# Seven products for eight: the up and gate projections of both feed-forwards formed from sums of weight blocks and of input halves

## The chip, the core and the metric

The kernel runs on one NeuronCore of one Trainium2 chip. The engines work side by side, each through its own program in order, and wait for one another on semaphores: TensorE (PE, matrix products), VectorE (DVE), ScalarE (ACT), GpSimd (POOL), and SyncE (SP), which issues most of the transfers from memory. The metric is the time of one execution in microseconds on the device; less is better.

## What is computed

The program is three blocks of a network on 512 tokens of width 1024, in f32. The change touches the gated feed-forward `conv_ffn`, which occurs twice (l = 0 after the gMLP mixer, l = 1 after the attention); the rest is left as it is. D_FF is 2816, so that `w_in` has 22 blocks of 128 columns for up and 22 for gate.

```python
def conv_ffn(h, w_in, conv_w, conv_b, w_down):
    a = h @ w_in
    C = a.shape[-1]
    a = lax.conv_general_dilated(
        a, conv_w[:, None, :].astype(a.dtype), window_strides=(1,),
        padding=[(CONV_WIDTH - 1, 0)], dimension_numbers=('NWC', 'WIO', 'NWC'),
        feature_group_count=C) + conv_b
    up, gate = jnp.split(a, 2, axis=-1)
    return (jax.nn.silu(gate) * up) @ w_down
```

Between them the kernel also computes, during the first feed-forward, the modulation vector of the third block, `mod = silu(c) @ ada_w + ada_b`, a product of one vector of 1024 with a matrix of 1024 by 6144.

## The kernel before

Activations are held turned: 128 channels on the partitions, 512 tokens along a row, `hT[:, k, :]` for the eight blocks k of 128 input channels (KB = 8). A **unit** n of a feed-forward (22 of them, FB = 22) is one block of 128 output channels of up and the same of gate. For each unit SP brings 1 MB of weights, in two transfers of 512 KB (`unit_loads`), into one of two slots of a ring; slot j = n mod 2. In the loops i counts pairs of units and j the unit in a pair, n = 2i + j. Waits go by counts, so that the order of each engine's program and the counts set all that happens.

- **PE** (`feed_forward` on `pe`, L910): per unit two products of 8 matmuls each, 128x128 weights against 512 columns, accumulated over k in bank 2j + b (b = 0 up, b = 1 gate). Each f32 matmul of the source is two MATMUL rows in the profile. Unit 0 is made by `raw_products` (L874) from the input before its norm is known. PE waits for the ring's load and for `ff_tap0`, which says that the bank was read two units ago. In l = 0, `ada_unit` (L839) follows each unit: two matmuls of one column that finish modulation unit n - 1.
- **ACT** (L1657, L1664): per bank the middle tap of the convolution with scale and bias, from PSUM to `conv`; then, for a pair of units, the two silu of the gates into `sil`.
- **DVE** (L2059, L2064, L2072): per bank the two outer taps, which multiply the shifted bank and add into `conv`; then gate times up into `act`. L2107 adds the bias to the two columns of modulation.
- **POOL** (`ada_unit`, L661, L663): in l = 0 only. For each of 24 modulation units it waits for a load of 1 MB, multiplies it by silu(c) broadcast (L661, 128x2048), and adds the eight blocks in a tree (L663, 1024, 512, 256 columns). Nothing of the feed-forward itself runs on POOL.
- **SP** (L443, L461): per unit the two ring transfers, once PE has freed the slot, and in l = 0 the modulation weights, once PE has made `ada_unit(n - 2)`.

After the units comes the down projection (L849, `linear`), whose first block waits for `act` block by block and whose blocks 0, 2 and 4 are followed by the last three modulation units.

## Time and profile before

| | us |
|---|---|
| median of 3 runs | 2788.99 |
| lowest, highest | 2786.19, 2789.99 |
| the profiled execution | 2788.59 |
| its span, first to last instruction | 2786.5 |
| PE busy in the span | 2626.5 (94%) |
| DVE, ACT, POOL busy | 842.5, 581.8, 442.4 |
| matmuls of L910 (both feed-forwards, units 1 to 21) | 582.1 |

The profile of one execution records every instruction with its start and length. "Busy" is the share of time in which an engine has an instruction in it. Matmuls are pipelined: the length of one (592 ns at 512 columns) is longer than the distance from one to the next, which is what counts and is read from a stretch of many. A small share of matmul records can be missing. Each row says what its engine waited for when it sat idle before.

### The profile page before, as it was taken

The numbers are of one execution on the slowest core, as the hardware profiler recorded it, in microseconds if no ns is written. First come the engines' busy times: TensorE is split into PE (matmuls) and PEld (weight loads), VectorE is DVE, ScalarE is ACT, GpSimd is POOL, SyncE is SP. The second block draws the span as 40 slices with busy tenths as digits, with TensorE's granted clock in tenths as the row PEclk, the third lists the DMA queues.
The fourth block names the chain that finished last, engine by engine and source line by source line (L and its number), as shares of the span: only waits on it lengthen the run. The fifth ranks groups of instructions, "written<-read, shape, count | busy, mean of one in ns | idle before, by whom it ended". The sixth has DMA issues, their size and how long they took to land. (4 is left out here: it accounts for less than half of the span.)

```text
span 2786.5 us, 27348 instructions
## 1 busy us (share of the span) xinstructions
PE 2626.5 (94%) x9893; PEld 1364.1 (49%) x9893; DVE 842.5 (30%) x1970; ACT 581.8 (21%) x1086; POOL 442.4 (16%) x403
## 2 busy tenths in 40 slices
PE   6999999999999999999999989999999999999992
PEld 6554444444566444444445446567655444444440
DVE  1023222102333232221022335565633323322215
ACT  2111111101333211110024542222113111111111
POOL 3015555400000100000112101011100111111110
PEclk9999999999999999999999999999998999999996
DMA  7224555432122122223322111000115799999985
GB/s 158 70 76 137 149 151 151 138 83 66 46 61 61 61 76 75 75 75 83 83 65 82 53 40 35 25 16 15 38 49 228 288 421 413 386 409 407 394 349 218
DMA packets 290655, 404.48 MB, mean 145 GB/s; under 512 B 14418, under 2 KB 253736, under 8 KB 264432
## 3 DMA queue, kind: packets, MB, share of 16 engines
q1 hardware_dynamic: 273808, 366.24, 38.1%
q0 software_dynamic: 15632, 34.44, 3.8%
q10 hardware_dynamic: 1104, 2.31, 0.2%
q8 instruction: 71, 1.16, 0.2%
q14 instruction: 40, 0.33, 0.0%
HBM read 396.20 MB, written 27.71 MB: 152 GB/s over the span
## 5 line engine op out<-in xcount | busy, mean ns | idle before, releaser
L910 PE MATMUL bank<-hT,bring 128*128 128x512 f32 x1344 | 582.1, 593 | 0.0
L910 PEld LDWEIGHTS bank<-hT,bring 128*128 128x128 f32 x1344 | 253.8, 190 | 311.9 <-issue 311.9
L849 PE MATMUL bank<-bring 128*128 128x512 f32 x704 | 303.3, 593 | 0.0
L1554 PE MATMUL bank<-bring 128*64 128x512 f32 (+1 forms) x512 | 226.8, 596 | 1.1 <-ACT bring L1974 0.8
L849 PEld LDWEIGHTS bank<-bring 128*128 128x128 f32 x704 | 133.5, 190 | 166.5 <-issue 166.5
L2059 DVE SCALAR_TENSOR_TENSOR ffw<-bank,col,ffw 128x511 f32<-128x511 f32 x88 | 65.9, 749 | 413.6 <-ACT ffw L1657 413.4
L1657 ACT ACTIVATE ffw<-bank,col 128x512 f32<-128x512 f32 x88 | 68.4, 777 | 492.8 <-PE bank L910 470.1
L2044 DVE TENSOR_TENSOR xT<-bank,xT 128x512 f32<-128x512 f32 x32 | 22.1, 692 | 370.5 <-PE bank L849 370.4
L1554 PEld LDWEIGHTS bank<-bring 128*64 128x64 f32 (+1 forms) x512 | 77.9, 157 | 96.2 <-issue 96.2
L1567 PE MATMUL bank<-bring,xT 128*64 128x512 f32 (+1 forms) x256 | 117.2, 600 | 5.7 <-DMA two<-exp_w_down 3.1
L646 POOL TENSOR_TENSOR ysq<-ysq 128x512 f32<-128x512 f32 x23 | 29.2, 1270 | 582.1 <-ACT ysq L1629 516.7
L1113 PE MATMUL bank<-hT,bring 128*128 128x512 f32 x256 | 115.8, 599 | 2.2 <-DVE ysq L2217 2.2
L1989 ACT ACTIVATE xT<-bank 128x256 f32<-128x256 f32 x44 | 16.9, 384 | 467.6 <-PE bank L1554 467.6
L1554 PE MATMUL bank<-two,bring 128*64 128x512 f32 (+1 forms) x256 | 113.4, 596 | 0.1
L1554 PE MATMUL bank<-ysq,bring 128*64 128x512 f32 (+1 forms) x256 | 113.4, 596 | 0.0
L740 POOL TENSOR_TENSOR ffw<-two,maskT 128x512 f32<-128x512 f32 x40 | 52.2, 1313 | 383.6 <-DVE two L2391 316.3
L2603 DVE TENSOR_TENSOR xT<-bank,ysq 128x512 f32<-128x512 f32 x88 | 60.8, 691 | 170.7 <-PE bank L1567 170.7
L661 POOL TENSOR_TENSOR two<-two,csil 128x2048 f32<-128x2048 f32 x24 | 86.5, 3603 | 155.6 <-DMA two<-ada_w 138.4
L663 POOL TENSOR_TENSOR two<-two 128x1024 f32<-128x1024 f32 (+2 forms) x72 | 104.0, 1444 | 5.7
L1208 PE MATMUL bank<-hT,bring 128*128 128x512 f32 x192 | 92.4, 617 | 2.4 <-ACT bring L1849 2.4
L2599 DVE TENSOR_TENSOR xT<-bank,xT 128x256 f32<-128x256 f32 x44 | 18.7, 424 | 239.1 <-ACT xT L1989 239.1
L792 POOL DMA_INDIRECT y_dram<-xT,slot_row x44 | 43.9, 998 | 203.1 <-DVE xT L2603 194.4
(498 smaller groups left out, 3603.1 us busy)
## 6 DMA issues: line engine op xcount, KB each, us to landing
bring<-f_w_in SPq DMA_DIRECT2D x88, 512.0 KB, 5.2
bring<-exp_w_gate SPq DMA_DIRECT2D x32, 1024.0 KB, 11.3
bring<-exp_w_up SPq DMA_DIRECT2D x32, 1024.0 KB, 18.4
bring<-exp_w_down SPq DMA_DIRECT2D x32, 1024.0 KB, 20.4
two<-ada_w SPq DMA_DIRECT2D x24, 1024.0 KB, 5.3
bring<-f_w_down SPq DMA_DIRECT2D x16, 1408.0 KB, 7.0
two<-exp_w_gate SPq DMA_DIRECT2D x16, 1024.0 KB, 10.9
two<-exp_w_up SPq DMA_DIRECT2D x16, 1024.0 KB, 18.1
```

Of the source, the lines that this page charges most:

```text
L661: step(1, nc.gpsimd.tensor_tensor(w, w, csil[:].unsqueeze(2).to_broadcast([P, KB, 256]), ALU.mult))
L663: step(k, nc.gpsimd.tensor_tensor(w[:, 0:n, :], w[:, 0:n, :], w[:, n:2 * n, :], ALU.add))
L740: nc.gpsimd.tensor_tensor(Am[h], ABT[h][:, :, 0:P], bc4(maskT[n][:]), ALU.mult)\
L849: mm = pe.matmul(ps[BANKS[stage][n % 4]][:], w[:, k, n % per * P:(n % per + 1) * P], rhs[:, k, :], start=(k == 0), stop=(k == kb - 1))
L910: mm = pe.matmul(ps[2 * j + b][:], w[:, k, b * P:(b + 1) * P], hT[:, k, :], start=(k == 0), stop=(k == KB - 1))
L1113: mm = pe.matmul(ps[n % 2][:], slot(n // 2, 8, 256)[:, k, n % 2 * P:(n % 2 + 1) * P], hT[:, k, :], start=(k == 0), stop=(k == KB - 1))
L1208: mm = pe.matmul(ps[(0, 7, 6)[m]][:], w, hT[:, k, :], start=(k == 0), stop=(k == KB - 1))
L1554: mm = pe.matmul(ps[3][m * h:m * h + m, :].rearrange("p (m n) -> p m n", m=2), hgT[par][:, k, m * h:m * h + m], w, start=(k == 0), stop=(k ...
L1567: mm = pe.matmul(ps[5 + half][m * h:m * h + m, :], eactT[par][:, k * P + m * h:k * P + m * h + m], exw[b][:, 4096 + k * D + half * 512:409 ...
L1657: nc.scalar.activation(conv[j][b], ps[2 * j + b][:], ACT.Identity, scale=col[:, bass.ds(c0 + P + blk, 1)], bias=col[:, bass.ds(c0 + P + 44 ...
L2059: nc.vector.scalar_tensor_tensor(out=c[:, 1:T], in0=ps[2 * j + b][:, 0:T - 1], scalar=col[:, bass.ds(c0 + 44 + blk, 1)], in1=c[:, 1:T], op ...
L2603: return nc.vector.tensor_tensor(yrow[par][:, cols], ps[5 + half][:], g2_row[:, cols], ALU.mult)
```

## The change

The 22 up and gate blocks keep their units. From unit 2 on, a unit's product is taken as a 2 by 2 product of blocks: the weights are split by input channels (k 0 to 3, k 4 to 7) and by up and gate, the inputs by input channels and by halves of the tokens (0 to 255, 256 to 511). Seven products of such blocks stand for the eight, each of 4 matmuls of 128x128 weights against 256 columns (`product`). Units 0 and 1 are made as before. What is new for this:

- `tsum`: four sums of input blocks (128x1024 each), made once per feed-forward by DVE, kept in a part of `ysq`.
- `wsum7`: four sums of weight blocks (128x512 each), made for every unit by POOL in `weight_sums`, in two buffers by j.
- PE's unit: 8 matmuls into bank a, 4 into d, 8 into b, 8 into c (two sets of four banks by j, `BANKS7`); it waits for the unit's weight sums (`ff_sum`) and for the bank set (`ff_step`).
- ACT copies the first product to SBUF (`p1_sb`); DVE makes up and gate in SBUF (`full`, in `AR2`) with seven adds of 256 columns; the taps of ACT and DVE then read `full` and not PSUM.
- The multiplication of the modulation weights by silu(c) moves from POOL to ACT (`ada_scale`, eight instructions of 256 columns with a scale per partition), at the end of each unit of l = 0. POOL keeps the tree.
- SP frees a ring slot after bank d, the second of the four.

The diff, cut: lines that go away on PE, ACT and DVE are those printed above.

```diff
+        tsum = [ysq[:, 1024 * n:1024 * n + 1024].rearrange("p (k t) -> p k t", k=4) for n in range(4)]
+        wsum7 = [[ysq[:, KB * T + 2048 * j + 512 * n:KB * T + 2048 * j + 512 * n + 512].rearrange("p (k n) -> p k n", k=4)
+                  for n in range(4)] for j in range(2)]
+        p1_sb, u2, u3 = rstd[:, 0:256], rms[:, 0:256], rms[:, 256:512]
...
+        full = [AR2[:, 0:512], AR2[:, 512:1024]]
...
+        FF_PRODS, FF_STEPS = 4 + 4 * (FB - 2), 8 + 9 * (FB - 2)
+        prods_at = lambda l, p: FF_PRODS * l + 4 + 4 * p
+        steps_at = lambda l, p: FF_STEPS * l + 8 + 9 * p
+        ADA_LATE = 2
+        acted_at = lambda l, p: 8 + 5 * p if l == 0 else 8 + 5 * (FB - 2) + ADA_LATE + 6 + 4 * p
+        BANKS7 = ((5, 4, 6, 7), (0, 3, 1, 2))
...
+                            if stage in ("f0in", "f1in"):
+                                sp.wait_ge(S[used], base + 2 + 2 * j if isinstance(i, int) else base + 8 * i - 10 + 4 * j)
...
-            def ada(i, first):
-                for j in range(2):
-                    ada_unit(2 * i + j, j)
-            def ada_unit(u, j):
-                def step(k, ins):
-                    ins.then_inc(s("ada_summed"), 1)
-                    if k < 4:
-                        settle(pool, s("ada_summed"), 4 * u + k)
+            def ada_unit(u, j, acted):
                 w = adaw[j]
-                settle(pool, s(f"ada{j}_loaded"), 16 * (u // 2) + 16 if isinstance(u, int) else 8 * (u - j) + 16)
-                step(1, nc.gpsimd.tensor_tensor(w, w, csil[:].unsqueeze(2).to_broadcast([P, KB, 256]), ALU.mult))
-                for k, n in ((2, 4), (3, 2), (4, 1)):
-                    step(k, nc.gpsimd.tensor_tensor(w[:, 0:n, :], w[:, 0:n, :], w[:, n:2 * n, :], ALU.add))
+                settle(pool, s("ff_acted"), acted)
+                for k, n in enumerate((4, 2, 1)):
+                    if k:
+                        settle(pool, s("ada_summed"), 3 * u + k)
+                    nc.gpsimd.tensor_tensor(w[:, 0:n, :], w[:, 0:n, :], w[:, n:2 * n, :], ALU.add).then_inc(s("ada_summed"), 1)
+            def weight_sums(l, i, j):
+                p = 2 * i + j - 2
+                _, base, d, *_ = plan[f"f{l}in"]
+                settle(pool, (S["ring0_loaded"], S["ring1_loaded"])[j], base[j] + 16 * d[j] * (i + 1))
+                if isinstance(p, int) and p < 2:
+                    pool.wait_ge(s("norm_ss_ready"), nth(f"f{l}"))
+                else:
+                    settle(pool, s("ff_prod"), prods_at(l, p - 2) + 4)
+                w, (s1, s2, s3, s4) = slot(j, 8, 256), wsum7[j]
+                at = 4 * ((FB - 2) * l + p)
+                nc.gpsimd.tensor_tensor(s1, w[:, 0:4, P:], w[:, 4:8, P:], ALU.add).then_inc(s("ff_sum"), 1)
+                nc.gpsimd.tensor_tensor(s3, w[:, 0:4, 0:P], w[:, 0:4, P:], ALU.subtract).then_inc(s("ff_sum"), 1)
+                settle(pool, s("ff_sum"), at + 1)
+                nc.gpsimd.tensor_tensor(s2, s1, w[:, 0:4, 0:P], ALU.subtract).then_inc(s("ff_sum"), 1)
+                settle(pool, s("ff_sum"), at + 3)
+                nc.gpsimd.tensor_tensor(s4, w[:, 4:8, 0:P], s2, ALU.subtract).then_inc(s("ff_sum"), 1)
+            def weight_side(l):
+                def body(i):
+                    for j in range(2):
+                        weight_sums(l, i, j)
+                        if l == 0:
+                            ada_unit(2 * i + j, j, acted_at(0, 2 * i + j - 2) + 5)
+                body(1)
+                with pool.Fori(2, FB // 2) as i:
+                    body(i)
...
-            looped(pool, ADA // 2, ada)
+            ada_unit(0, 0, 1)
+            ada_unit(1, 1, 8)
+            weight_side(0)
             for u in range(ADA, ADA_UNITS):
-                ada_unit(u, u % 2)
...
+                def product(bank, half, weights, rhs):
+                    for k in range(4):
+                        mm = pe.matmul(ps[bank][:, 256 * half:256 * half + 256], weights[:, k, :], rhs[:, k, :],
+                                       start=(k == 0), stop=(k == 3))
+                    return mm
+                def body(i):
                     for j in range(2):
+                        p = 2 * i + j - 2
+                        a, d, b, c = BANKS7[j]
+                        w, (s1, s2, s3, s4), (t1, t2, t3, t4) = slot(j, 8, 256), wsum7[j], tsum
                         ring_ready(pe, stage, i, j)
...
+                        pe.wait_ge(s("ff_sum"), 4 * ((FB - 2) * l + p) + 4)
+                        if not isinstance(p, int):
+                            pe.wait_ge(s("ff_step"), steps_at(l, p - 2) + 7)
+                        elif p == 0:
+                            pe.wait_ge(s("ff_step"), FF_STEPS * l + 4)
+                        else:
+                            pe.wait_ge(s("ff_tap0"), 44 * l + 4)
+                        product(a, 0, w[:, 0:4, 0:P], hT[:, 0:4, 0:256])
+                        product(a, 1, w[:, 4:8, 0:P], hT[:, 4:8, 0:256]).then_inc(s("ff_prod"), 1)
+                        if l == 0:
+                            ada_unit(2 * i + j - 1, 1 - j, ps[d][:, 256:258])
+                        product(d, 0, w[:, 4:8, P:], t4).then_inc(s("ff_prod"), 1)
+                        product(b, 0, s2, t2)
+                        product(b, 1, s3, t3).then_inc(s("ff_prod"), 1)
+                        product(c, 0, s1, t1)
+                        product(c, 1, s4, hT[:, 4:8, 256:512]).then_inc(s("ff_prod"), 1)
...
+                def ada_scale(u, j):
+                    settle(act_e, s(f"ada{j}_loaded"), 16 * (u // 2) + 16 if isinstance(u, int) else 8 * (u - j) + 16)
+                    for k in range(KB):
+                        ins = nc.scalar.activation(adaw[j][:, k, :], adaw[j][:, k, :], ACT.Copy, scale=csil[:, k:k + 1])
+                    ins.then_inc(s("ff_acted"), 1)
+                def middle_tap(src, j, b, blk):
+                    nc.scalar.activation(conv[j][b], src, ACT.Identity,
+                                         scale=col[:, bass.ds(c0 + P + blk, 1)],
+                                         bias=col[:, bass.ds(c0 + P + 44 + blk, 1)]).then_inc(s("ff_acted"), 1)
+                def gate(n, j):
+                    settle(act_e, s("ff_tap0"), 44 * l + 2 * n + 2)
+                    nc.scalar.activation(sil[j], conv[j][1], ACT.Silu).then_inc(s("ff_acted"), 1)
...
+                def body(i):
                     for j in range(2):
+                        n = 2 * i + j
+                        p = n - 2
+                        settle(act_e, s("ff_prod"), prods_at(l, p) + 1)
+                        if not isinstance(p, int) or p > 0:
+                            settle(act_e, s("ff_step"), steps_at(l, p - 1) + 2)
+                        nc.scalar.copy(p1_sb, ps[BANKS7[j][0]][:, 0:256]).then_inc(s("ff_acted"), 1)
+                        settle(act_e, s("ff_step"), steps_at(l, p) + 7)
+                        settle(act_e, s("ff_act"), FB * l + n - 1)
                         for b in range(2):
...
+                            middle_tap(full[b], j, b, n + 22 * b)
+                        gate(n, j)
+                        if l == 0:
+                            ada_scale(n, j)
...
+                h = [[hT[:, 4 * r:4 * r + 4, 256 * c:256 * c + 256] for c in range(2)] for r in range(2)]
+                s0 = FF_STEPS * l
+                dve.wait_ge(s("norm_h_ready"), h_count(f"f{l}", KB - 1))
+                nc.vector.tensor_tensor(tsum[0], h[0][1], h[0][0], ALU.subtract).then_inc(s("ff_step"), 1)
+                nc.vector.tensor_tensor(tsum[2], h[1][1], h[0][1], ALU.subtract).then_inc(s("ff_step"), 1)
+                dve.wait_ge(s("ff_step"), s0 + 1)
+                nc.vector.tensor_tensor(tsum[1], h[1][1], tsum[0], ALU.subtract).then_inc(s("ff_step"), 1)
+                dve.wait_ge(s("ff_step"), s0 + 3)
+                nc.vector.tensor_tensor(tsum[3], tsum[1], h[1][0], ALU.subtract).then_inc(s("ff_step"), 1)
...
+                def body(i):
                     for j in range(2):
...
+                        n = 2 * i + j
+                        p = n - 2
+                        a, d, b, c = [ps[x] for x in BANKS7[j]]
+                        prod, step, acted = prods_at(l, p), steps_at(l, p), acted_at(l, p)
+                        up, gate = full
+                        lo, hi = slice(0, 256), slice(256, 512)
+                        settle(dve, s("ff_acted"), acted + 1)
+                        nc.vector.tensor_tensor(up[:, lo], p1_sb, a[:, hi], ALU.add).then_inc(s("ff_step"), 1)
+                        settle(dve, s("ff_prod"), prod + 3)
+                        nc.vector.tensor_tensor(u2, p1_sb, b[:, lo], ALU.add).then_inc(s("ff_step"), 1)
+                        settle(dve, s("ff_step"), step + 2)
+                        nc.vector.tensor_tensor(u3, u2, b[:, hi], ALU.add).then_inc(s("ff_step"), 1)
+                        settle(dve, s("ff_step"), step + 3)
+                        nc.vector.tensor_tensor(gate[:, lo], u3, d[:, lo], ALU.subtract).then_inc(s("ff_step"), 1)
+                        if l == 0:
+                            ada_unit(n - 1, d[:, 256:258])
+                        settle(dve, s("ff_prod"), prod + 4)
+                        nc.vector.tensor_tensor(up[:, hi], u2, c[:, lo], ALU.add).then_inc(s("ff_step"), 1)
+                        nc.vector.tensor_tensor(gate[:, hi], u3, c[:, lo], ALU.add).then_inc(s("ff_step"), 1)
+                        settle(dve, s("ff_step"), step + 5)
+                        nc.vector.tensor_tensor(up[:, hi], up[:, hi], c[:, hi], ALU.add).then_inc(s("ff_step"), 1)
+                        settle(dve, s("ff_step"), step + 7)
+                        for b2 in range(2):
+                            outer_taps(full[b2], n, j, b2, acted + 2 + b2, step + 8 + b2)
+                        gated(n, j, acted + 4)
```

Unit n waits on POOL for `ff_acted` at `acted_at(0, n - 2) + 5`, that is 8 + 5(n - 2) + 5. ACT counts one up for the copy, two for the middle taps, one for the silu and one for the last instruction of `ada_scale(n)`: five a unit, 8 before unit 2.

**POOL, the loop of the first feed-forward.** Before, one unit (names: `two` holds the modulation weights, `csil` silu(c)):

```order
L661 TENSOR_TENSOR two<-two,csil 128x2048 [waits consts,ada0_loaded]
L52 ISA
L663 TENSOR_TENSOR two<-two 128x1024 [waits consts,ada_summed]
L52 REGISTER_ALU
L663 TENSOR_TENSOR two<-two 128x512 [waits consts,ada_summed]
L52 REGISTER_ALU
L663 TENSOR_TENSOR two<-two 128x256 [waits consts,ada_summed]
```

And now, one unit and the beginning of the next (`bring` holds the ring, `ysq` the weight sums):

```order
L694 TENSOR_TENSOR ysq<-bring 128x512 [waits consts,ff_prod]
L695 TENSOR_TENSOR ysq<-bring 128x512
L52 ISA
L697 TENSOR_TENSOR ysq<-ysq,bring 128x512 [waits consts,ff_sum]
L52 REGISTER_ALU
L699 TENSOR_TENSOR ysq<-bring,ysq 128x512 [waits consts,ff_sum]
L52 ISA
L681 TENSOR_TENSOR two<-two 128x1024 [waits consts,ff_acted]
L52 ISA
L681 TENSOR_TENSOR two<-two 128x512 [waits consts,ada_summed]
L52 REGISTER_ALU
L681 TENSOR_TENSOR two<-two 128x256 [waits consts,ada_summed]
```

What was a wait for a transfer ahead of L661 is a wait for ACT ahead of L681, and the weight sums of the next unit (L694 again) stand behind it.

**ACT, the first feed-forward.** Before, units 0 and 1 and the beginning of the loop (`ffw` holds `conv` and `sil`), with nothing between the silu and the next unit's taps:

```order
L1657 ACTIVATE ffw<-bank,col 128x512 [waits raw_scaled,ff_prod] x2
L1657 ACTIVATE ffw<-bank,col 128x512 [waits ff_prod] x2
L1664 ACT_TABLE_LOAD
L1664 ACTIVATE ffw<-ffw 128x512 [waits ff_tap0] x2
L80 UNCONDITIONAL_BRANCH
L80 ISA
L52 ISA [waits consts,ff_prod]
L1657 ISA [waits consts,ff_act]
L1657 ACTIVATE ffw<-bank,col 128x512
```

Now, unit 2, ahead of the loop (`rstd` is `p1_sb`, `AR2` is `full`):

```order
L1757 COPY rstd<-bank5 128x256 [waits ff_prod]
L1728 ACTIVATE ffw<-AR2,col 128x512 [waits ff_act,ff_step]
L1728 ACTIVATE ffw<-AR2,col 128x512
L1734 ACTIVATE ffw<-ffw 128x512 [waits ff_tap0]
L1724 ACTIVATE two<-two,csil 128x256 [waits ada0_loaded]
L1724 ACTIVATE two<-two,csil 128x256 x7
```

The scaling of the modulation weights (L1724) has come in behind the silu of the same unit.

**PE, the loop of the first feed-forward.** Before, one unit:

```order
L906 ISA [waits ring0_loaded]
L910 MATMUL bank<-hT,bring 128x512 [waits ff_tap0]
L910 MATMUL bank<-hT,bring 128x512 x7
L906 REGISTER_ALU
L910 MATMUL bank<-hT,bring 128x512 [waits ff_tap0]
L910 MATMUL bank<-hT,bring 128x512 x7
L836 ISA
L839 MATMUL bank<-onec,two 128x1 [waits mod_ready,ada_summed]
L839 MATMUL bank<-onec,two 128x1
```

Now, one unit:

```order
L968 ISA [waits ring0_loaded]
L970 ISA [waits ff_sum]
L958 MATMUL bank<-hT,bring 128x256 [waits ff_step]
L958 MATMUL bank<-hT,bring 128x256 x7
L884 ISA
L887 MATMUL bank<-onec,two 128x1 [waits mod_ready,ada_summed]
L887 MATMUL bank<-onec,two 128x1
L958 MATMUL bank<-ysq,bring 128x256 x4
L958 MATMUL bank<-ysq 128x256 x12
L958 MATMUL bank<-hT,ysq 128x256 x4
```

PE's first product of a unit has gained a wait for POOL (`ff_sum`), and the 16 matmuls of 512 columns have become 28 of 256.

## Rows read from the trace of the kernel before

**Rows 1.** The page: each engine's busy time (share) and instructions.

```profile
PE 2626.5 (94%) x9893; PEld 1364.1 (49%) x9893; DVE 842.5 (30%) x1970; ACT 581.8 (21%) x1086; POOL 442.4 (16%) x403
```

**Rows 2.** Timeline, PE, first feed-forward: start, length, line, count of merged rows.

```profile
233.60 0.50 PE L839 MATMUL bank<-onec,two 128*128 128x1 f32 x4
233.96 13.98 PE L910 MATMUL bank<-hT,bring 128*128 128x512 f32 x32
...
517.56 19.13 PE L849 MATMUL bank<-bring 128*128 128x512 f32 x44
```

**Rows 3.** Timeline, second feed-forward, ACT: the same bank of two units.

```profile
1050.85 0.78 ACT L1657 ACTIVATE ffw<-bank,col 128x512 f32<-128x512 f32 x1 [5.96 <-PE bank L910]
...
1064.59 0.78 ACT L1657 ACTIVATE ffw<-bank,col 128x512 f32<-128x512 f32 x1 [5.95 <-PE bank L910]
```

**Rows 4.** Timeline, PE, matmuls of 256 columns; in brackets idle time before, releaser.

```profile
32.44 27.79 PE L944 MATMUL bank<-bring,ysq 128*128 128x256 f32 x128
69.84 16.19 PE L944 MATMUL bank<-bring,ysq 128*128 128x256 f32 x64 [9.61 <-DMA bring<-a_w_in]
```

**Rows 5.** Windows: stretch, then PE, PEld, DVE, ACT, POOL busy, PEclk, DMA, GB/s.

```profile
64.00:64.50 0.50, 0.00 (x0) 0.00 (x0) 0.00 (x0) 0.00 (x0) 0.00 (x0) 0.50 1.05 156
...
73.50:74.00 0.50, 0.50 (x3) 0.41 (x2) 0.00 (x0) 0.00 (x0) 0.00 (x0) 0.50 0.00 0
...
74.50:75.00 0.50, 0.50 (x4) 0.45 (x3) 0.00 (x0) 0.00 (x0) 0.00 (x0) 1.00 0.00 0
...
1427.00:1428.00 1.00, 1.00 (x6) 1.00 (x7) 0.00 (x0) 0.00 (x0) 0.00 (x0) 0.50 0.00 0
```

**Rows 6.** Groups, DVE and ACT: shapes, count | busy, mean ns | idle before.

```profile
L2599 DVE TENSOR_TENSOR xT<-bank,xT 128x256 f32<-128x256 f32 x44 | 18.7, 424 | 239.1 <-ACT xT L1989 239.1
...
L1657 ACT ACTIVATE ffw<-bank,col 128x512 f32<-128x512 f32 x88 | 68.4, 777 | 492.8 <-PE bank L910 470.1 <-PE bank L874 11.3 <-DVE bank L2038 11.3
...
L1664 ACT ACTIVATE ffw<-ffw 128x512 f32<-128x512 f32 x44 | 27.3, 624 | 26.0 <-DVE ffw L2064 26.0
...
L1994 ACT COPY xT<-bank 128x256 f32<-128x256 f32 x44 | 16.4, 372 | 13.1 <-PE bank L1560 13.1
...
L1712 ACT ACTIVATE bring<-bank,ss 128x256 f32<-128x256 f32 x16 | 7.6, 473 | 56.3 <-PE bank L944 56.2
```

**Rows 7.** Timeline, DVE in the second feed-forward's loop: outer taps, gate times up.

```profile
1051.77 0.75 DVE L2059 SCALAR_TENSOR_TENSOR ffw<-bank,col,ffw 128x511 f32<-128x511 f32 x1 [5.10 <-ACT ffw L1657]
1052.66 0.75 DVE L2064 SCALAR_TENSOR_TENSOR ffw<-bank,col,ffw 128x510 f32<-128x510 f32 x1
...
1054.23 0.69 DVE L2072 TENSOR_TENSOR bring<-ffw 128x512 f32 x1 [0.22 <-ACT ffw L1664]
```

**Rows 8.** Timeline, ACT: two instructions back to back, SBUF to SBUF.

```profile
931.81 0.70 ACT L1631 ACTIVATE two<-xT,col 128x512 f32<-128x512 f32 x1
932.42 0.61 ACT L1629 ACTIVATE ysq<-xT 128x512 f32<-128x512 f32 x1
```

**Rows 9.** Timeline, POOL in the first feed-forward: scaling, then the tree of three.

```profile
240.11 3.61 POOL L661 TENSOR_TENSOR two<-two,csil 128x2048 f32<-128x2048 f32 x1 [6.19 <-DMA two<-ada_w]
243.80 4.49 POOL L663 TENSOR_TENSOR two<-two 128x1024 f32<-128x1024 f32 x3
```

**Rows 10.** Group, POOL: an add of two 128x512 blocks in SBUF.

```profile
L646 POOL TENSOR_TENSOR ysq<-ysq 128x512 f32<-128x512 f32 x23 | 29.2, 1270 | 582.1 <-ACT ysq L1629 516.7 <-ACT ysq L1932 64.7
```

**Rows 11.** Timeline, DVE beside POOL in the third block.

```profile
1708.53 1.26 DVE L2401 TENSOR_TENSOR ysq<-two,maskT 128x512 f32<-128x512 f32 x1
1709.82 1.64 DVE L2402 TENSOR_TENSOR ysq<-ysq,ident 128x512 f32<-128x512 f32 x1
1711.38 0.68 DVE L2403 TENSOR_TENSOR ysq<-ysq,ident 128x512 f32<-128x512 f32 x1
...
1707.98 2.93 POOL L740 TENSOR_TENSOR ffw<-two,maskT 128x512 f32<-128x512 f32 x2 [3.16 <-DVE two L2391]
```

**Rows 12.** The page, transfers issued: count, KB each, median us to landing.

```profile
bring<-f_w_in SPq DMA_DIRECT2D x88, 512.0 KB, 5.2
```

More of the change, by code:

```diff
@@ L2077, in feed_forward @@
+                body(1)
+                with dve.Fori(2, FB // 2) as i:
+                    body(i)
                 add_linear(f"f{l}dn", {1: ADA - 1, 3: ADA, 5: ADA + 1} if l == 0 else {})
```

159 lines of the change are left out of this document (87 added, 72 removed).

## The prediction

> **What bounds the kernel now.** I read the page first: PE is busy 94% of the span and every other engine 30% or less [rows 1]. Then the timeline of PE in the first feed-forward. Twenty units (2 to 21) lie between the matmuls that begin at 233.96 and those of the down projection at 517.56 [rows 2]: 283.6 us, 14.18 a unit, with no idle time in it. In the second feed-forward, without the modulation matmuls, the same bank comes round after 1064.59 - 1050.85 = 13.74 us [rows 3]. So PE sets the pace in both, and the other engines follow it with room to spare. A change there gains what it takes from PE, as long as no other engine's work has to be waited for; that is the question here.
>
> **PE's own part.** A unit had 16 matmuls of 512 columns, now 28 of 256, which is 7/8 of the columns. Each is two instructions, so 56 a unit. The price of one of 256 columns is read from a stretch of 128: 27.79 us less some 0.4 for the length of the last, over 127, is 0.216 us [rows 4]. 56 x 0.216 = 12.1 us. Against 13.74 that is 1.64 us less a unit, at most 33 us for 20 units of one feed-forward. The weight loads double in number per column, but at 256 columns that same stretch has them and keeps its 0.216, so they cost nothing more.
>
> **The first feed-forward: a new chain.** Here the order decides. POOL works in order. Behind the weight sums of unit n it waits for ACT to have scaled modulation unit n, and only behind that tree come the weight sums of unit n + 1. ACT scales at the end of unit n, behind its silu, which wants the taps, which want up and gate of unit n, which want PE's last product of unit n. And PE's first product of unit n + 1 waits for its weight sums. This closes a ring through PE, DVE, ACT and POOL: nothing of unit n + 1 can start on PE while the tail of unit n runs. Before, POOL waited for a transfer alone, and PE was never held. The gap from PE's last matmul to its next first one, step by step:
> - three adds of 256 columns on DVE, one wait behind the other: 0.42 each as in L2599 [rows 6], with 0.15 for each hand-over: 1.7;
> - ACT's middle tap of up: 0.78 as L1657 [rows 6], with 0.1: 0.9 (the tap of gate runs beside DVE);
> - DVE's four outer taps, 0.89 from start to start, 0.75 the last [rows 7], 0.15 to begin: 3.6;
> - silu of gate: 0.62 [rows 6] and 0.1: 0.7;
> - ACT's eight scalings of 256 columns. The trace has none of this form. Nearest from SBUF, 0.70 at 512 columns with a scale, next start after 0.61 [rows 8]; at 256 from PSUM 0.37 plain and 0.47 with a scale [rows 6], less the 0.1 by which neighbours overlap. Bounds 0.27 and 0.50 each; I take 0.40, near the row with a scale: 3.3 with the wait;
> - POOL's tree, 4.49 [rows 9], with 0.1: 4.6;
> - POOL's four weight sums at 1.27 [rows 10], with 0.2 for two waits: 5.3;
> - PE's start: 0.2.
>
> Together 20.3 us (bounds 18.3 with the cheap scalings and no hand-overs to 22.5 with dear scalings and slow register waits in the loop). PE's part is 12.1, plus 0.4 for the modulation matmuls (14.18 - 13.74 = 0.44 now) and 0.2 for the last result to come out: 12.7.
>
> **The clock.** PE idles 20 us in every 33. After 9.6 us of idling [rows 4] the granted clock stood at 0.50 (1.2 GHz) from 64.0 on, and still at 73.5, though PE worked again from 69.8; at 74.5 it was 1.00 (2.4 GHz) [rows 5]. So some 4.3 us of work ran at half clock. The stretch of 64 then took 16.19 us where 63 x 0.216 + 0.4 = 14.0 would do: 2.2 us lost [rows 4]. I take 2.2 for every gap; bounds 1.5 and 3.5, since in another place, behind light work, a half clock lasted over 6 us (a row of it is shown, 1427) [rows 5].
>
> Period 12.7 + 20.3 + 2.2 = 35.2 us, against 14.18: 21.0 more. There are 20 such gaps, the first ahead of unit 2 (POOL waits there for the scaling of unit 1, at the end of ACT's first two units, a like tail) and none behind unit 21, whose tail is covered by the 19.1 us of the first down block [rows 2]: **+420 us**. SP's loads have room in this: a ring transfer lands 5.2 us after its issue [rows 12].
>
> **The second feed-forward.** No modulation, hence no ring: POOL's sums for unit n + 2 wait for PE to have finished unit n, take 5.3 us, and are wanted 12.1 us later. A slot is freed after 12 of 28 matmuls (5.2 us), loaded by 10.4, summed by 17.4 (the sums wait until 12.1), wanted at 24.2. DVE's work per unit is seven adds (7 x 0.57 = 4.0), the wait for ACT's tap 0.9, taps 3.6, silu 0.7, gate times up 0.9: 10.1 us, under 12.1, so hidden with 2.0 us to spare. Cover gone, every us more than that would count twenty times. One thing eats it: the taps now have both inputs in SBUF, `full` and `conv`, and so has POOL's add. In the third block a DVE operation of that kind, 0.68 us alone (L2403), took 1.26 and 1.64 beside POOL's adds, and POOL's two took 2.93 instead of 2.5 [rows 11]. POOL's sums begin when PE ends a unit and DVE's taps 2.6 us later, so the taps meet about two of four adds: 2.5 us, 0.5 over the cover. Once DVE runs late it meets fewer, so I take 0.2 us a unit, 4 us: **-33 + 4 = -29 us**. The input sums (four of 1024 columns on DVE) lie beside the 13.7 us of PE's unit 1.
>
> **Sum**, against the profiled execution's own 2788.6, which is 0.4 below the median of the runs: 2788.6 + 420 - 29 = **3180 us**, 14% slower. With the bounds: gap 18.3 to 22.5 gives -40 to +44, the clock -14 to +26. I round to 3120 and 3250.
>
> **Rivals.**
>
> *Wait on ACT does not bind (the other side).* One mechanism: the scaling and the tree for unit n would be done while PE still works, as the load was before. Then POOL needs 4.6 + 5.3 = 9.9 us a unit, under PE's 12.5, and PE bounds both: -33 - 29 = -62, 2727 us. It needs the awaited count to be reached a unit earlier than I count. Against it: both diff and order put the scaling behind the silu of the same unit, and five counts a unit with eight ahead fit the wait exactly. The point from which it decides: the change breaks even at a period of 14.18 + 29/20 = 15.6 us, so a gap of 2.9 us without any loss of clock; POOL's weight sums alone, which stand in the ring, are 5.3. Chance 4%.
>
> *Clock stays down.* If the work between the gaps did not bring the clock back, all 56 matmuls would run at half clock: 12.1 us lost a gap and not 2.2, 20 x 9.9 = 198 more, 3378 us. Against it: 4.3 us of the very same kind of work did bring it back [rows 4, 5]. Chance 5%. The Trainium skill (TensorE: Matmul & The Clock Gate, in its caveats on the trace of the gate) says that the clock has been seen to hang low for long; no stretch here shows that.
>
> *DVE and POOL shut one another out in the second feed-forward.* If each of the four POOL adds holds up one of DVE's taps in full, DVE's unit is 10.1 + 4 x 1.27 = 15.2 us, over PE's, and over the 13.74 of before: +29 and not -29, 3238 us. Rows 11 show the mechanism; that it strikes four times a unit, always, is against it, since DVE would drift out of phase. Chance 9%. The Trainium skill (SBUF — State Buffer, Who interferes with whom) states it as a rule: a DVE instruction with two SBUF inputs and a GpSimd instruction that reads SBUF exclude each other for a whole instruction. By that rule at its worst this rival's 3238 is the time; the lengths in rows 11 agree with the rule.
>
> **How the numbers follow.** Forecast 82%, DVE against POOL 9%, clock 5%, no binding wait 4%. The range of 3120 to 3250 holds the forecast's bounds and the DVE rival, and leaves out the other two and what my steps may have missed. A measurement of this kernel tells some 0.2% from no change. Faster: 4%, the wait that doesn't bind. Within 0.2%: 1%. Slower: 95%.
>
> **What the profile of the changed kernel would show.** PE idle for some 20 us ahead of each unit of the first feed-forward, put down to POOL L699; POOL in turn waiting for ACT L1724 at L681. Per period eight L1724 of about 0.4, a tree of 4.5, four sums of 1.27. The granted clock at 0.50 in the gaps and about 4 us beyond. In the second feed-forward PE without idle time and 12.1 to 12.4 us a unit, L2160 and L2164 with maxima well over 0.75. I am wrong if PE's gap there is under 15 us, if its idle time is put down to a load, or if the second feed-forward's units take over 13.7 us.

## The result and the profile after

The changed kernel took 3157.69 us (median of 4 runs, 3155.58 to 3158.35), against 2789.49 us (4 runs, 2786.19 to 2790.95) for the kernel before beside it: a ratio of 1.132 [1.130, 1.134], 13.2% slower. The forecast was 3180, its range 3120 to 3250.

The page of the changed kernel: busy time of each engine, and the granted clock in 40 slices of the span.

```profile
PE 2618.7 (83%) x10853; PEld 1581.0 (50%) x10853; DVE 992.3 (31%) x2258; ACT 673.1 (21%) x1318; POOL 566.8 (18%) x539
...
PEclk9996776676689999999999999999999899999996
```

PE had 94% of the span [rows 1] and has 83%. The busy time is almost the same (2626.5 and 2618.7 us); what grew is idle time, and it lies in one stretch, slices 4 to 12 of the 40, where the mean granted clock is 0.6 to 0.8: the first feed-forward. The page's groups name who ends the idle time of PE and of POOL there (busy, mean ns, idle before, releaser):

```profile
L958 PE MATMUL bank<-hT,bring 128*128 128x256 f32 x640 | 193.9, 470 | 377.3 <-POOL ysq L699 343.0
...
L681 POOL TENSOR_TENSOR two<-two 128x1024 f32<-128x1024 f32 (+2 forms) x72 | 104.5, 1453 | 542.1 <-ACT two L1724 521.2
```

PE waited 343 us for POOL's last weight sum (L699), and POOL 521 us for ACT's scaling (L1724). The timeline of one gap shows the whole ring in the order of time (start, length, engine, line; in brackets the idle time before and its releaser):

```profile
398.05 1.89 PE L958 MATMUL bank<-hT,ysq 128*128 128x256 f32 x8
399.98 0.42 DVE L2214 TENSOR_TENSOR AR<-rms,bank 128x256 f32<-128x256 f32 x1 [2.05 <-PE bank L958]
...
401.37 1.52 ACT L1728 ACTIVATE ffw<-AR,col 128x512 f32<-128x512 f32 x2 [9.96 <-DVE AR L2217]
402.33 0.75 DVE L2160 SCALAR_TENSOR_TENSOR ffw<-AR,col,ffw 128x511 f32<-128x511 f32 x1 [1.27 <-ACT ffw L1728]
...
404.78 0.75 DVE L2164 SCALAR_TENSOR_TENSOR ffw<-AR,col,ffw 128x510 f32<-128x510 f32 x1
405.57 0.63 ACT L1734 ACTIVATE ffw<-ffw 128x512 f32<-128x512 f32 x1 [2.68 <-DVE ffw L2164]
406.10 3.28 ACT L1724 ACTIVATE two<-two,csil 128x256 f32<-128x256 f32 x8
...
409.46 4.48 POOL L681 TENSOR_TENSOR two<-two 128x1024 f32<-128x1024 f32 x3 [24.86 <-ACT two L1724]
...
417.67 1.26 POOL L699 TENSOR_TENSOR ysq<-bring,ysq 128x512 f32<-128x512 f32 x1
```

Each begins where what it waits for ends. PE's last matmul of the unit ends at 399.94, and its next begins at 419.08:

```profile
419.08 6.01 PE L958 MATMUL bank<-hT,bring 128*128 128x256 f32 x16 [19.14 <-POOL ysq L699]
453.18 6.03 PE L958 MATMUL bank<-hT,bring 128*128 128x256 f32 x16 [19.01 <-POOL ysq L699]
```

The period is 34.1 us (34.2 on the mean of the 19), 19.1 of it idle. The windows of that gap (stretch, busy times, then the granted clock):

```profile
400.00:403.00 3.00, 0.00 (x0) 0.00 (x0) 1.73 (x4) 1.52 (x2) 0.00 (x0) 1.00 0.00 0
...
404.00:419.00 15.00, 0.00 (x0) 0.00 (x0) 2.08 (x3) 3.82 (x9) 9.24 (x7) 0.50 0.00 0
419.00:423.00 4.00, 3.92 (x9) 3.20 (x10) 0.00 (x0) 0.00 (x0) 0.00 (x0) 0.50 0.00 0
...
424.00:426.00 2.00, 2.00 (x13) 1.82 (x12) 0.34 (x1) 0.37 (x1) 0.00 (x0) 1.00 0.00 0
```

PE, idle since 399.94, was granted the full clock (2.4 GHz) until at least 403, then half of it (1.2 GHz), and still had half at 423, 3.9 us after it had begun to work again. Sixteen matmuls took 6.01 us there and take 3.7 at the full clock.

In the second feed-forward there is no ring and no idle time. Two units of PE, and DVE's taps beside POOL's sums:

```profile
1510.74 3.62 PE L958 MATMUL bank<-hT,bring 128*128 128x256 f32 x16
...
1522.83 3.62 PE L958 MATMUL bank<-hT,bring 128*128 128x256 f32 x16
```

```profile
1513.28 0.76 DVE L2160 SCALAR_TENSOR_TENSOR ffw<-AR,col,ffw 128x511 f32<-128x511 f32 x1 [1.25 <-ACT ffw L1728]
1513.43 1.73 POOL L697 TENSOR_TENSOR ysq<-ysq,bring 128x512 f32<-128x512 f32 x1
1514.18 1.53 DVE L2164 SCALAR_TENSOR_TENSOR ffw<-AR,col,ffw 128x510 f32<-128x510 f32 x1
...
1515.24 1.59 POOL L699 TENSOR_TENSOR ysq<-bring,ysq 128x512 f32<-128x512 f32 x1
1515.63 1.75 DVE L2160 SCALAR_TENSOR_TENSOR ffw<-AR,col,ffw 128x511 f32<-128x511 f32 x1
```

The unit is 12.09 us, against 13.74 [rows 3]. Two of four taps (the multiply-adds of the convolution) are held by POOL's adds (1.53 and 1.75 instead of 0.75), and POOL's adds by the taps (1.73 and 1.59 instead of 1.26).

**The ledger**, from the two timelines of PE: the first feed-forward's units 2 to 21 took 680.4 us instead of 283.6 (+396.8), the second's 20 units 33 less. Unit 2's turn came 2.4 us earlier, and behind the second feed-forward the third block took 5.4 us more and the experts 2.4 more. The sum is +369, as the spans say (3155.6 and 2786.5).

### The profile page after: what moved, and what is told of

Same layout as the page of the kernel before. It is cut to its first block and busy times, and to the rows that moved or that the text cites. A ratio compares the mean times of both kernels' runs of the same rounds, so it can differ in the third digit from the quotient of the medians.

```text
span 3155.6 us, 30751 instructions
## 1 busy us (share of the span) xinstructions
PE 2618.7 (83%) x10853; PEld 1581.0 (50%) x10853; DVE 992.3 (31%) x2258; ACT 673.1 (21%) x1318; POOL 566.8 (18%) x539
## 3 DMA queue, kind: packets, MB, share of 16 engines
q1 hardware_dynamic: 273808, 366.24, 33.6%
## 5 line engine op out<-in xcount | busy, mean ns | idle before, releaser
L958 PE MATMUL bank<-hT,bring 128*128 128x256 f32 x640 | 193.9, 470 | 377.3 <-POOL ysq L699 343.0
L958 PEld LDWEIGHTS bank<-hT,bring 128*128 128x128 f32 x640 | 153.8, 244 | 414.2 <-issue 385.3
L958 PE MATMUL bank<-ysq 128*128 128x256 f32 x960 | 213.7, 379 | 0.0
L681 POOL TENSOR_TENSOR two<-two 128x1024 f32<-128x1024 f32 (+2 forms) x72 | 104.5, 1453 | 542.1 <-ACT two L1724 521.2
L958 PEld LDWEIGHTS bank<-ysq 128*128 128x128 f32 x960 | 182.4, 190 | 24.8
L2204 DVE TENSOR_TENSOR AR<-rstd,bank 128x256 f32<-128x256 f32 x40 | 16.7, 418 | 373.9 <-ACT rstd L1757 373.9
L1728 ACT ACTIVATE ffw<-AR,col 128x512 f32<-128x512 f32 x80 | 60.8, 806 | 306.7 <-DVE AR L2217 306.7
L1188 PE MATMUL bank<-hT,bring 128*128 128x512 f32 x256 | 117.4, 606 | 2.2 <-DVE ysq L2365 2.2
L2160 DVE SCALAR_TENSOR_TENSOR ffw<-AR,col,ffw 128x511 f32<-128x511 f32 x80 | 79.2, 989 | 49.2 <-ACT ffw L1728 49.2
L1283 PE MATMUL bank<-hT,bring 128*128 128x512 f32 x192 | 92.4, 617 | 2.4 <-ACT bring L1954 2.4
```

The lines of the kernel that those rows point to most:

```text
L681: nc.gpsimd.tensor_tensor(w[:, 0:n, :], w[:, 0:n, :], w[:, n:2 * n, :], ALU.add).then_inc(s("ada_summed"), 1)
L958: mm = pe.matmul(ps[bank][:, 256 * half:256 * half + 256], weights[:, k, :], rhs[:, k, :], start=(k == 0), stop=(k == 3))
L1188: mm = pe.matmul(ps[n % 2][:], slot(n // 2, 8, 256)[:, k, n % 2 * P:(n % 2 + 1) * P], hT[:, k, :], start=(k == 0), stop=(k == KB - 1))
L1283: mm = pe.matmul(ps[(0, 7, 6)[m]][:], w, hT[:, k, :], start=(k == 0), stop=(k == KB - 1))
L1728: nc.scalar.activation(conv[j][b], src, ACT.Identity, scale=col[:, bass.ds(c0 + P + blk, 1)], bias=col[:, bass.ds(c0 + P + 44 + blk, 1)]). ...
L2160: nc.vector.scalar_tensor_tensor(out=c[:, 1:T], in0=src[:, 0:T - 1], scalar=col[:, bass.ds(c0 + 44 + blk, 1)], in1=c[:, 1:T], op0=ALU.mult ...
```

## Experiments

The theory: the ring over PE, DVE, ACT and POOL holds PE in the first feed-forward, and the time is its length. Four rivals: the added load on POOL and DVE is the cost, whatever the order (the load theory); the new tail of a unit, adds, taps and silu in SBUF, holds PE by itself (the tail theory); the clock is a large part of the gap's price; DVE and POOL shut each other out.

e1, e2, e4, e5, e6 and e8 were run once each. The kernel before, run nine times beside e9, spread over 5.5 us (0.2%), so a difference of some us against a single run says little.

**Weight sums ahead of the tree (e1).** In POOL's loop the sums of unit n + 1 come before the tree of unit n, and the ends of the loop change to match:

```diff
                         weight_sums(l, i, j)
                         if l == 0:
-                            ada_unit(2 * i + j, j, acted_at(0, 2 * i + j - 2) + 5)
+                            if isinstance(i, int) and j == 0:
+                                ada_unit(1, 1, ADA1_SCALED)
+                            else:
+                                ada_unit(2 * i + j - 1, 1 - j, acted_at(0, 2 * i + j - 3) + SCALED)
```

> The changed kernel, with POOL's order in the first feed-forward altered: the weight sums of unit n stand ahead of the modulation tree of unit n - 1 and no longer behind it; ACT is left as it is. Ring theory (PE is held by POOL's order behind ACT's scaling): the sums are off the ring, but PE's modulation matmuls of unit n - 1, which stand behind the first eight matmuls of unit n, still wait for the tree. Scaling ends 9.4 us after PE's last matmul, the tree 4.5 later, so PE stops in mid-unit until 14.1; then 0.4 + 8.7 us of matmuls: 23.2 us a unit, 25.4 with 2.2 for the half clock, against 34.1. Time 2940 to 2985, I take 2980. Tail theory (the three DVE adds, taps and silu in SBUF hold PE by themselves, whatever POOL's order): no change, 3158. Load theory (POOL's amount of work sets the unit): no change, 3158.

Measured: 2994.46 us (before 2788.76). The first product is free of the ring now, and the ring closes at the next thing that waits for POOL, the modulation matmuls, which stand behind the unit's first sixteen:

```profile
418.35 3.28 ACT L1728 ACTIVATE two<-two,csil 128x256 f32<-128x256 f32 x8
421.71 4.48 POOL L682 TENSOR_TENSOR two<-two 128x1024 f32<-128x1024 f32 x3 [17.35 <-ACT two L1728]
...
426.24 1.01 PE L891 MATMUL bank<-onec,two 128*128 128x1 f32 x4 [10.60 <-POOL two L682]
```

163 us less with the same instructions: load alone, or the tail alone, doesn't set this time. It came out 14 us over the ring's 2980 and outside its range: the unit is 26.0 us on the mean and not 25.4. With 12.5 us of PE's work at the full clock (e9) and 10.5 of idle time, that leaves 2.9 us for the clock and not 2.2.

**Scaling ahead of the taps' tail (e2).** ACT scales modulation unit n right behind its copy of the unit's first product, ahead of the middle taps and the silu (the counts awaited by POOL and DVE move with it):

```diff
+                        if l == 0:
+                            ada_scale(n, j)
                         settle(act_e, s("ff_step"), steps_at(l, p) + 7)
...
                         gate(n, j)
-                        if l == 0:
-                            ada_scale(n, j)
```

> The changed kernel, with only ACT's order altered: the eight scalings of unit n stand right behind the copy of its first product, ahead of taps and silu (those of unit 1 behind the taps of unit 0); POOL's order is as in the changed kernel. Ring theory: the ring is now PE's first product, copy, scaling 3.3, tree 4.5, sums 5.1, 17.4 us a unit warm; the sums fall beside the taps (0.8 more) and PE idles some 5 us a unit, so that part of a unit runs at half clock: 18 to 20 us a unit. Time 2838 to 2875, I take 2865. Tail theory: the tail of up and gate is as long as before, no change beyond the 3.3 us of scaling that leave it: 3090. Load theory: 3158.

Measured: 2876.03 us, 11 over what was taken and 1 over the range. The gap fell from 19.1 to 4.7 us, the period to 20.5 (18 to 20 were expected):

```profile
412.37 6.67 PE L958 MATMUL bank<-hT,bring 128*128 128x256 f32 x16 [4.74 <-POOL ysq L699]
...
432.84 6.67 PE L958 MATMUL bank<-hT,bring 128*128 128x256 f32 x16 [4.72 <-POOL ysq L699]
```

With 4.7 us of idle time the clock still fell: sixteen matmuls took 6.67 us and not 3.62. The tail theory, with its 3090, falls here.

**Both (e3).** The two edits together.

> Both edits at once: scalings behind the copy, weight sums of unit n ahead of the tree of unit n - 1. Ring theory: nothing that PE waits for hangs on the same unit any more; sums of unit n + 1 are made in the first 5 to 7 us of unit n, scaling ends 7.3 us after its start, the tree at 11.9, before PE's 12.5 are over. PE without idle time at 12.5 us a unit in the first feed-forward, 12.1 in the second, clock at 1.00: 2789 - 33 - 33 = 2723, faster than both kernels by 2.4%. Tail theory: 3090 or more. Load theory (POOL's 9.5 us a unit and DVE's 3.7 us with two SBUF inputs exclude one another, 13.2 in all, over PE's 12.5): 2737.

Measured in four runs: 2743.27 us (2741.28 to 2743.5), before 2788.76, ratio 0.983 [0.981, 0.985]: 1.7% faster than the kernel before, by an order of the same instructions. But it is 20 us over the 2723 of the ring theory, and nearer to the load theory's 2737, whose unit of 13.2 us is also nearer to what the timeline shows than 12.5:

```profile
412.78 0.61 PE L891 MATMUL bank<-onec,two 128*128 128x1 f32 x4 [0.33 <-POOL two L682]
...
413.20 1.75 DVE L2164 SCALAR_TENSOR_TENSOR ffw<-AR,col,ffw 128x511 f32<-128x511 f32 x1
...
420.82 4.91 POOL L682 TENSOR_TENSOR two<-two 128x1024 f32<-128x1024 f32 x3 [1.38 <-ACT two L1728]
...
425.78 0.61 PE L891 MATMUL bank<-onec,two 128*128 128x1 f32 x4 [0.20 <-POOL two L682]
```

The tree again ends just behind the time at which PE wants it, since the taps (held by POOL's sums) delay the silu and ACT's scaling behind it. The period is 13.0 and 13.1 in turn. So with the order mended the load counts after all: POOL's sums at 1.6 to 1.7 us each, its tree at 4.9 and its wait of 1.4 us for ACT's scaling fill its 13 us. Beside that, the start of the loop costs 3.0 us of idle time and 2.9 more by the clock, once.

**Scaling twice (e4).** Eight plain copies of the modulation weights onto themselves ahead of the eight scalings, so ACT's step in the ring is doubled; the values are unchanged:

```diff
+                    for k in range(KB):
+                        ins = nc.scalar.copy(adaw[j][:, k, :], adaw[j][:, k, :])
+                    ins.then_inc(s("ff_acted"), 1)
+                    settle(act_e, s("ff_acted"), copied)
+                    for k in range(KB):
```

> The changed kernel, with one suspected cost doubled: ahead of each scaling of a modulation unit ACT copies its eight blocks onto themselves, eight instructions more of 256 columns. ACT is busy 5.8 us of 34 a unit. Ring theory: the copies lie on the ring, 20 periods x 3.3 to 3.5 us = 66 to 70 more: 3224 to 3228. Any theory in which ACT's scaling runs beside other work: 3158.

Measured: 3209.66 us, 52 more than the changed kernel.

```profile
455.31 2.53 ACT L1724 COPY two<-two 128x256 f32<-128x256 f32 x8
457.87 3.30 ACT L1728 ACTIVATE two<-two,csil 128x256 f32<-128x256 f32 x8
```

Plain copies took 2.56 us from start to start and not 3.3; 20 x 2.56 = 51. The added time goes through to the result in full, though ACT is busy for a fifth of the span. The miss is in the length of a copy, not in the ring.

**Scaling on POOL, as before (e5).** The seven products stay; the modulation weights are scaled by one POOL instruction of 2048 columns and ACT has no part in it:

```diff
-                settle(pool, s("ff_acted"), acted)
-                for k, n in enumerate((4, 2, 1)):
...
+                nc.gpsimd.tensor_tensor(w, w, csil[:].unsqueeze(2).to_broadcast([P, KB, 256]), ALU.mult).then_inc(s("ada_summed"), 1)
+                for k, n in ((1, 4), (2, 2), (3, 1)):
```

> The changed kernel with one part undone: the scaling of the modulation weights goes back to POOL (one instruction of 2048 columns, 3.6 us), ahead of the tree, where it waits for a transfer alone; sums of unit n, then scaling and tree of unit n. Ring theory: no ring is left. POOL's own work is 3.6 + 4.5 + 5.1 + 0.2 = 13.4 us a unit, over PE's 12.5; with DVE's taps and gate times up (3.7 us with two SBUF inputs) shut out in full it is 17.1. So 13.4 to 17.1 us a unit against 14.18 of the kernel before: 2741 to 2814, I take 2793. Tail theory: near 3090.

Measured: 2783.64 us, before 2791.65 (0.3%, in a single run). The ring is open, and POOL itself is the bound: its unit, from one L677 to the next, is 15.03 us without idle time, and that and 9.3 us of idle time ahead of the loop eat most of the second feed-forward's gain:

```profile
403.56 3.60 POOL L677 TENSOR_TENSOR two<-two,csil 128x2048 f32<-128x2048 f32 x1
403.84 5.40 PE L958 MATMUL bank<-hT,bring 128*128 128x256 f32 x16 [2.36 <-POOL ysq L698]
404.03 3.67 DVE L2152 SCALAR_TENSOR_TENSOR ffw<-AR,col,ffw 128x511 f32<-128x511 f32 x1 [1.42 <-ACT ffw L1728]
...
418.59 3.60 POOL L677 TENSOR_TENSOR two<-two,csil 128x2048 f32<-128x2048 f32 x1
...
433.97 3.72 PE L958 MATMUL bank<-hT,bring 128*128 128x256 f32 x16 [2.40 <-POOL ysq L698]
```

So moving the scaling to ACT takes 3.6 us a unit off POOL, which this kernel needs; it was the place in ACT's order that cost. The tap of 0.75 us took 3.67: it ended 0.54 us after POOL's instruction of 3.60 did. The two rows of PE differ in the clock: behind 2.36 us of idle time sixteen matmuls took 5.40 us, at a granted clock of 0.50 from 406 to 408, and behind 2.40 us they took 3.72. So this kernel pays for the clock too, in some of its units.

**The gap filled with dummy matmuls (e6, e8).** Behind the products of each unit of the first feed-forward PE does 74 (e6) or 84 (e8) matmuls of 250 columns whose result nobody reads, to keep it busy in the gap (37 in the source in e6, 42 in e8, as each is two instructions):

```diff
+                        if l == 0:
+                            for _ in range(37):
+                                pe.matmul(ps[BANKS7[1 - j][1]][:, 260:510], ident[:], hT[:, 0, 0:250], start=True, stop=True)
```

> The changed kernel, with 37 matmuls of 250 columns (74 instructions, some 15.7 us) added behind each unit of the first feed-forward, into columns of a bank that nobody reads; they fill most of PE's gap of 19.1 us and end before its wait does. Clock theory (each gap costs about 2.4 us because PE comes back at half clock): the clock stays at 1.00, the period falls from 34.1 to 31.7, 20 x 2.4 = 48 less: 3110. If the gap costs no more than the wait itself: 3158. If the added work itself got in the way: more than 3158.

Measured: 3150.70 us, 7 less than the changed kernel and not 48. Two kinds of period follow one another in it:

```profile
412.32 5.40 PE L958 MATMUL bank<-hT,bring 128*128 128x256 f32 x16 [3.57 <-POOL ysq L699]
445.85 3.72 PE L958 MATMUL bank<-hT,bring 128*128 128x256 f32 x16 [3.44 <-POOL ysq L699]
477.81 5.40 PE L958 MATMUL bank<-hT,bring 128*128 128x256 f32 x16 [3.56 <-POOL ysq L699]
```

The one that begins with the clock up takes 31.96 us, the one before it 33.53. 3.0 to 3.6 us of idle time were left, and behind 13 of 19 such gaps the clock fell, about 1 us after PE had begun again: behind the row at 412.32 the windows read (PE busy, granted clock)

```profile
413.00:414.00 1.00, 1.00 (x6) 0.72 0.00 0
414.00:415.00 1.00, 1.00 (x4) 0.50 0.00 0
```

And the dummies behind the last unit cover nothing: they stand before the down projection and cost their whole 15 us. I had overlooked this. So e6 did not decide between the theories, and e8 leaves fewer us idle:

> The same as e6_busy_gap, with 84 dummy matmuls after each half unit's real ones in the first feed-forward instead of 74, so that 1.3 to 1.5 us of PE's idle are left of a gap of 19.1 us instead of 3.4 to 3.6; the output is unchanged. In e6_busy_gap the 6 periods that began with the clock up were 31.8 to 32.0 us long and the others 33.5 to 33.7, against 34.1 in the changed kernel. If the clock is what makes the rest of PE's work longer (2.4 us of each period), all 20 periods are now 31.8 to 32 us, 20 x 2.2 = 44 us less than the changed kernel: 3112 us (3106 to 3120), and the granted clock stays at 1.00 through the first feed-forward. If something else makes the first matmuls after the gap long (their late weights, or the start after a wait), most periods stay at 33.5 us and the time at 3148 to 3152 us.

Measured: 3126.19 us (before 2788.66), 6 us outside what was expected.

```profile
439.67 3.72 PE L958 MATMUL bank<-hT,bring 128*128 128x256 f32 x16 [1.32 <-POOL ysq L699]
...
867.07 17.87 PE L986 MATMUL bank<-hT,ident 128*128 128x250 f32 x84
884.78 19.05 PE L897 MATMUL bank<-bring 128*128 128x512 f32 x44
```

From the third on, the periods are 31.8 or 32.0 us (the first, behind the gap ahead of the loop that nothing fills, is still 33.6). The 19 take 607.4 us (247.02 to 854.44) against 649.6 in the changed kernel: 2.2 us each is the clock. The last two rows are the overlooked 17.7 us. Without them e8 would be at 3108.5: an estimate, not a run.

**The sums twice, in the second feed-forward (e7).** Ahead of its four sums POOL makes four more adds of the same size, whose results are overwritten, where no ring exists:

```diff
+                if l == 1:
+                    at = 4 * (FB - 2) + 8 * p
+                    for k, x in enumerate((s1, s3, s2, s4)):
+                        nc.gpsimd.tensor_tensor(x, w[:, 0:4, P:], w[:, 4:8, P:], ALU.add).then_inc(s("ff_sum"), 1)
...
```

> The changed kernel, with POOL's four weight sums of each unit of the second feed-forward made twice (eight adds of 128x512, the first four are overwritten): POOL 10.3 us a unit where PE's unit is 12.1. Exclusion theory (a DVE instruction with two SBUF inputs and a POOL add never run at the same time): POOL and DVE together need 8 x 1.27 + 4 x 0.75 + 0.69 = 13.8 us a unit, the second feed-forward grows to 13.8 to 14.2 a unit, 20 x 1.9 = 38 more: 3195. If they only slow one another a little, or not: POOL's 10.3 stay under 12.1 and the time is 3158.

Measured in four runs: 3166.59 us (3164.27 to 3169.48), 9 more than the changed kernel: neither value, though nearer to the one without exclusion. Over a whole unit of it:

```profile
1507.39 3.71 PE L964 MATMUL bank<-hT,bring 128*128 128x256 f32 x16
1507.64 5.93 POOL L697 TENSOR_TENSOR ysq<-bring 128x512 f32<-128x512 f32 x4 [0.39 <-PE bank L964]
...
1520.09 3.72 PE L964 MATMUL bank<-hT,bring 128*128 128x256 f32 x16 [0.35 <-POOL ysq L705]
```

Units of 12.2 and 12.7 us in turn, 12.43 on the mean, where POOL's eight adds fill the time. At the start of the loop PE lost some 4 us more, once: 2.3 of idle time, behind which the clock fell, and 1.8 by the clock. The rival's mechanism is real, but three taps are held, by 0.8 to 1.0 us each (2.5 together), not four by 1.27. So at twice POOL's adds 1.3 of the 1.65 us a unit are still gained; what more adds would do was not run.

**The modulation matmuls one product later (e9).** From e3: the matmuls that wait for the tree go behind PE's second product, 2 us later; the count that tells DVE of that product is now given by the next matmul:

```diff
                         if l == 0:
...
+                            product(d, 0, w[:, 4:8, P:], t4)
                             ada_unit(2 * i + j - 1, 1 - j, ps[d][:, 256:258])
-                        product(d, 0, w[:, 4:8, P:], t4).then_inc(s("ff_prod"), 1)
-                        product(b, 0, s2, t2)
...
+                        for k in range(4):
+                            mm = pe.matmul(ps[b][:, 0:256], s2[:, k, :], t2[:, k, :], start=(k == 0), stop=(k == 3))
+                            if l == 0 and k == 0:
+                                mm.then_inc(s("ff_prod"), 1)
```

> e3_both, with the conditioning matmuls (four of one column, which wait for GpSimd's tree of adds) moved behind PE's second product of the half unit, 2 us later in PE's order; the output is unchanged. In e3_both they made PE wait 0.20 and 0.33 us in alternate half units of the first feed-forward, the period being 13.13 and 13.00 us, while PE's own work is 12.65 to 12.7. If that wait is what holds PE, the period falls to 12.7 and the time by 19 x 0.35 = 6 to 7 us, from 2743 to 2737 us (2735 to 2740): the tree then ends later against the filter taps on DVE, which makes them shorter, and GpSimd's own work (6.7 + 4.9 = 11.7 us) fits. If GpSimd is full in e3_both (13.0 us with its wait of 1.4 us for ScalarE's scaling), the wait only moves to the first product, which waits for GpSimd's weight sums, and the time stays at 2743 us (2741 to 2745).

Measured in five runs: 2733.54 us (2732.66 to 2735.95), before 2788.48 (2786.62 to 2792.12), ratio 0.980 [0.979, 0.982]: the fastest version, 10 us under e3 and under both expected ranges. Successive units:

```profile
413.22 3.62 PE L962 MATMUL bank<-hT,bring 128*128 128x256 f32 x16
425.75 3.62 PE L962 MATMUL bank<-hT,bring 128*128 128x256 f32 x16
438.29 3.62 PE L962 MATMUL bank<-hT,bring 128*128 128x256 f32 x16
443.88 0.61 PE L891 MATMUL bank<-onec,two 128*128 128x1 f32 x4 [0.25 <-POOL two L682]
451.34 3.62 PE L962 MATMUL bank<-hT,bring 128*128 128x256 f32 x16
```

Three units of 12.53 us without a wait, then one with a short one: 12.66 on the mean, against 13.06 in e3. Neither theory is exact: the wait did hold PE, as the first said, but POOL is nearly full too, as the second said, since every fourth unit PE still waits. The period gives some 8 us of the 10. The rest is at the start of the loop, where the clock fell in e3, after 2.99 us of idle time, and did not in e9, after 2.90; e6 and e5 have gaps of nearly one length behind which it fell in some cases and not in others, so 0.09 us of idle time need not be the reason.

## Why the prediction was right

The forecast's case came about, and the sum was 22 us too high: +391 where the span shows +369. By its steps:

- **What bounds the kernel.** PE in both feed-forwards before, a ring through four engines in the first after. Right; e1, e2 and e4 each changed the ring alone, and the time followed: it missed what was expected by 14, 11 and some 16 us, in changes of 163, 282 and 52.
- **The gap**, 20.3 forecast: 19.1 measured. From the rows of the ring: DVE's three adds 1.1 and not 1.7 (they start 0.33 apart; 0.42 each and a hand-over of 0.15 each is what I had put); ACT's middle tap, to the start of the outer ones, 1.3 and not 0.9; the outer taps 3.2 and not 3.6; silu and scalings 3.9 and not 4.0; tree, sums and PE's start 9.6 and not 10.1. It was a sum of small hand-overs and durations, most a little too dear. Times 19, this is 23 us, the largest error of the sum.
- **The first gap** was 15.8 us and not 20.3: 4.5 us less. The prediction took a like tail there, but unit 1 is made in the old form, without the three adds.
- **The eight scalings**, 3.3 forecast between bounds of 2.2 and 4.0: 3.28. A single one has 492 ns, close to the upper bound of 0.50; back to back they start 0.40 apart. The overlap of neighbours [rows 8] was what decided.
- **PE's part and the clock**, 12.7 + 2.2 forecast: 34.2 - 19.1 = 15.1 measured, which over 20 periods is 4 us more. e8 gives the clock alone: 2.2. Right; the rival of a clock that stays down did not occur.
- **The second feed-forward**, -29 forecast: -33. The gain on PE was exact (12.09, against 12.1). The 0.2 us a unit for DVE and POOL was not needed: taps and sums met twice, as forecast, but that cost DVE 1.8 us and not 2.5, and it stayed within the cover, for DVE still idles 1.5 us a unit before its last adds.
- **The wait that does not bind**, the other side, needs the tree a unit earlier. That is e3 and e9, at 2743 and 2733 where this rival's sum said 2727. Its mechanism is sound in a kernel with another order; in this one the order forbade it.
- **What was not in the sum**: +5.4 us in the third block and +2.4 in the experts, whose code is unchanged. Only short stretches at the half clock lie elsewhere there. A row of the changed kernel and the same eight matmuls of the kernel before:

```profile
1822.91 5.38 PE L1188 MATMUL bank<-hT,bring 128*128 128x512 f32 x8
```

```profile
1459.60 3.68 PE L1113 MATMUL bank<-hT,bring 128*128 128x512 f32 x8
```

In e8, with the same code behind the first feed-forward, the whole rest took 4.1 us less than in the changed kernel (2239.6 and 2243.7). So some 4 us there can come and go with what lies ahead; why, and whether all 7.8 are of this kind, was not shown. Where unit 2's earlier turn (2.4 us) comes from was not looked into.

The errors partly cancel: -27 us from the gaps, -4 from the second feed-forward and -2 from unit 2's turn, against +4 from PE's part and +8 from the blocks behind. The mechanism is right; that the total is only 22 us off is in part luck.

## What to carry to other kernels

Before work is taken off the bounding engine, follow what each in-order engine has queued behind its new wait, and close the loop: if unit n + 1 of the first engine waits for the tail of unit n, the sum of the tail is the price of every unit, however idle these engines are (here busy 16 to 26% of the first feed-forward). The first cure is the order and not the amount: put what the next unit needs (the weight sums) ahead of what only this unit's side work needs (the tree), and start side work that needs nothing of the tail (the scaling) before the tail. Then look at the next wait: here the modulation matmuls still held PE by 10.5 us in e1 and by tenths of a us in e3. Once the ring is open the amount counts again (POOL's 15.03 us a unit in e5, its 13 in e3).
